# Layer 0 of a two-layer mixer and expert block: order of the output projection's column halves, and gathers in four buffers

## What is computed

```python
x = x + g1 * (concat(fourier, ssd) @ w_out)          # output projection, 1536 -> 1024, gated, residual
h2 = rms_norm(x) * (1 + sc2) + sh2
# PEER, for each token and each of 8 heads
q = h2 @ peer_wq                                     # two halves of 128
s = einsum(q, peer_keys); s_top, i_top = top_k(s, 16)
g_score, c_idx = top_k(s_top[0] + s_top[1], 16)      # 16 experts of 16384
act = gelu(u[experts] . h2) * softmax(g_score)
x = x + g2 * sum(act * v[experts])
```

## Time and profile before

| what | before |
|---|---|
| median of 3 runs | 4402.59 us (4401.46 to 4406.03) |
| the profiled execution | 4409.58 us, its span 4407.5 us |
| busy: TensorE, VectorE, ScalarE, GpSimd | 3129.8, 2860.7, 1122.0, 1587.9 us |
| bytes moved by the gathers | 1342.26 of 1471.78 MB |
| layer 0's first gather issued | at 720.9 us of the span |
| chain that ended last, largest share | DMA of experts, 13% |

### The profile page before, as it was taken

How to read it: one execution, slowest core, us unless ns; L and a number is a source line. 1 busy time by engine, 2 the same in 40 slices (tenths; PEclk the granted TensorE clock), 3 DMA queues, 4 the chain that set the end, 5 groups by cost and what they waited for, 6 DMA issues and landing times. The chain is left out here.

```text
span 4407.5 us, 37632 instructions
## 1 busy us (share of the span) xinstructions
PE 3129.8 (71%) x12112; PEld 1329.6 (30%) x12112; DVE 2860.7 (65%) x7084; ACT 1122.0 (25%) x2966; POOL 1587.9 (36%) x1383
## 2 busy tenths in 40 slices
PE   7999997676666765656666666999876755555555
PEld 4655554332222321111222222565432311111111
DVE  2524843988888887555555555565788899555554
ACT  1122521322322332111222211564322322111111
POOL 0002401545444444444444441001344454444443
PEclk9999998888887887776777878999987877777677
DMA  4114734999999999999999996103999999999998
GB/s 172 39 39 153 256 104 176 412 420 421 420 418 397 414 421 421 421 420 414 412 416 421 416 420 256 39 1 121 383 420 420 418 421 416 422 420 420 419 420 337
DMA packets 223656, 1471.78 MB, mean 334 GB/s; under 512 B 25436, under 2 KB 29244, under 8 KB 53220
## 3 DMA queue, kind: packets, MB, share of 16 engines
q0 software_dynamic: 184320, 1342.26, 73.5%
q1 hardware_dynamic: 37764, 123.17, 7.8%
q10 hardware_dynamic: 1376, 3.96, 0.2%
HBM read 1467.02 MB, written 2.28 MB: 333 GB/s over the span
## 5 line engine op out<-in xcount | busy, mean ns | idle before, releaser
L1868 PE MATMUL banks<-arena 128*64 128x512 f32 x5120 | 1688.5, 821 | 1206.0 <-ACT arena L2038 1148.9
L1670 POOL DMA_INDIRECT arena<-experts,arena x1280 | 1511.6, 1181 | 2309.8 <-PE banks L1868 1474.9
L2198 DVE CUSTOM_DVE_ANT_0 arena<-arena 128x1024 f32<-128x1024 f32 x1280 | 1535.4, 1224 | 793.1 <-DMA arena<-experts,arena 788.1
L1868 PEld LDWEIGHTS banks<-arena 128*64 128x64 f32 x5120 | 462.7, 187 | 2358.0 <-ACT arena L2038 1338.8
L2032 ACT ACTIVATE arena<-arena 128x4 f32<-128x4 f32 x320 | 66.0, 206 | 2334.3 <-DVE arena L2198 2319.4
L2038 ACT ACTIVATE arena<-arena 128x64 f32<-128x64 f32 x1280 | 340.6, 336 | 36.4
L1756 PE MATMUL banks<-arena 128*128 128x512 f32 (+3 forms) x960 | 289.0, 455 | 7.0 <-DMA arena<-wq 6.4
L434 PE MATMUL banks<-arena 128*128 128x512 f32 (+1 forms) x640 | 208.6, 486 | 1.8 <-PEq L201 1.8
L1756 PEld LDWEIGHTS banks<-arena 128*128 128x128 f32 x960 | 160.8, 191 | 113.3 <-issue 86.9
L870 POOL TENSOR_TENSOR arena<-arena 128x256 f32<-128x256 f32 x48 | 41.1, 856 | 423.6 <-POOLq L625 332.3
L1689 PE MATMUL banks<-arena 128*128 128x512 f32 x416 | 185.8, 600 | 2.3 <-PEq L953 1.5
(11 more groups left out here) (250 smaller groups left out, 3004.0 us busy)
## 6 DMA issues: line engine op xcount, KB each, us to landing
arena<-l_w_ada SPq DMA_DIRECT2D x48, 1024.0 KB, 5.0
arena<-wq SPq DMA_DIRECT2D x54, 512.0 KB
arena<-experts,arena POOLq DMA_INDIRECT x1280
arena<-l_w_in SPq DMA_DIRECT2D x7, 2048.0 KB, 7.8
arena<-l_w_out SPq DMA_DIRECT2D x4, 1536.0 KB, 8.9
arena<-l_w_o SPq DMA_DIRECT2D x4, 1024.0 KB, 9.9
arena<-keys SPq DMA_DIRECT2D x27, 128.0 KB
arena<-gates SPq DMA_DIRECT2D x6, 512.0 KB, 6.2
```

What stands on the lines that cost most here:

```text
L1670: pool.indirect_dma_start(slots[n], None, tbl, bass.IndirectOffsetOnAxis(ap=expert[:, ring[c], k:k + 1], axis=0)).then_inc(land[n]["sem"], ...
L1868: mm = pe.matmul(core["ps"][QS * j:QS * j + QS, c, :], diag[:, g % 2, k, :], v[:, D + c * 512:D + (c + 1) * 512], start=(g % (NB * PH) == ...
L2198: dve.tensor_tensor_reduce(u, u, rep[i // PH % 2][:, k % NQ, :], 1.0, 0.0, ALU.mult, ALU.add, dots[:, k:k + 1]).then_inc(dot["sem"], up(dot))
```

## The change

Only `peer_block` and its two tables change. The order of projection halves becomes a list, `project`, and `turn_of[t, c]` is a half's place in it. Layer 1's list is the old order, and its `spread_at` has a new meaning (start step for tile 0, for later tiles), which gives the same steps 4 and 5. In layer 0:

- halves run (0,0), (0,1), then the first halves of tiles 1 to 5, then the second halves of tiles 1 to 5;
- projections use PSUM banks 6 and 7 in turn, and the gate's transposes move to banks 2 to 5;
- the first 16 gathers use four slots only: three over the first column half's weights, and one that lies elsewhere. They wait for the first seven halves. From gather 16 on, 12 slots are used, and the 8 new ones wait for all halves, as before;
- `project(1, 1)` stands ahead of the loop on TensorE, and `project(2, 1)` to `project(5, 1)` after its steps 0 to 3, with the turned rows of tiles 1 to 4 behind them. `ask(2)` moves to step 1, `ask(3)` and `turn_rows(5)` to step 4;
- on VectorE the sums, norms and columns of tiles 1 to 5 move between the dot batches in the same way, and on ScalarE the squares, roots and columns;
- choices inside the loop begin at step 3 instead of 1; the spread of tile 1's rows is at steps 5 and 6 instead of 1 and 2.

```diff
@@ -1360,17 +1360,20 @@
-     "choose_from": 1, "spread_at": (1, 2), "small": 12, "ring_from": 0,
+     "choose_from": 3, "spread_at": (5, 1), "small": 4, "ring_from": 16,
+     "project": [(0, 0), (0, 1)] + [(t, 0) for t in range(1, TT)] + [(t, 1) for t in range(1, TT)],
      "rep": (L0 + 3072, L0 + 5120), "ht": HO,
-     "slots": [RO + n * ROWS for n in range(6)] + [L0] + [L0 + 7168 + n * ROWS for n in range(5)]},
+     "slots": [RO, RO + ROWS, RO + 2 * ROWS, L0 + 7168] + [RO + n * ROWS for n in range(3, 6)] +
+              [L0] + [L0 + 7168 + n * ROWS for n in range(1, 5)]},
...
@@ -1413,7 +1416,8 @@
-    REP_AT = m["spread_at"]
+    rep_at = {NB * PH * t + m["spread_at"][t > 0] + j: (t + 1, j) for t in range(tiles - 1) for j in range(NQ)}
+    turn_of = {tc: n for n, tc in enumerate(m["project"])}
...
@@ -1579,13 +1583,13 @@
-    def bank_of(c):
-
-        return c if layer == 0 else 6 + c
+    def bank_of(t, c):
+
+        return 6 + turn_of[t, c] % 2
     def spread_place(c):
 
-        return (3, 384 + 32 * c) if layer == 1 and c < EARLY else (6 + c % 2, 0)
+        return (3, 384 + 32 * c) if c < EARLY else (6 + c % 2, 0)
...
@@ -1645,10 +1649,10 @@
-                sp.wait_ge(free["sem"], at(free, max(used[n][1] for n in range(3)) + 1))
+                sp.wait_ge(free["sem"], at(free, max(used[n][1] for n in (0, 1, 2)) + 1))
...
@@ -1663,10 +1667,12 @@
                     uses, prev = before[u]
                     if uses:
                         pool.wait_ge(free["sem"], at(free, prev + 1))
-                    elif layer == 0 or n >= m["small"]:
+                    elif n >= m["small"]:
                         pool.wait_ge(omm["sem"], at(omm, 2 * tiles))
                         if layer == 0:
                             pool.wait_ge(oad["sem"], at(oad, 2 * tiles))
+                    elif layer == 0:
+                        pool.wait_ge(omm["sem"], at(omm, turn_of[tiles - 1, 0] + 1))
                     pool.indirect_dma_start(slots[n], None, tbl,
                                             bass.IndirectOffsetOnAxis(ap=expert[:, ring[c], k:k + 1], axis=0)
                                             ).then_inc(land[n]["sem"], up(land[n], 16))
...
-                elif layer == 1:
-                    pe.wait_ge(oad["sem"], at(oad, 2 * t + c - 1))
                 else:
-                    pe.wait_ge(oad["sem"], at(oad, 2 * (t - 1) + c + 1))
+                    pe.wait_ge(oad["sem"], at(oad, turn_of[t, c] - 1))
...
@@ -1812,54 +1825,59 @@
+                turn_rows(0)
+                project(2, 0, 0, 2)
+                pe.wait_ge(gca["sem"], at(gca, TT - 1))
+                pe.wait_ge(gcv["sem"], at(gcv, TT - 1))
+                query(0, 0)
+                query(0, 1)
+                project(2, 0, 2, 3)
+                scores(0, 0)
+                scores(0, 1)
+                project(2, 0, 3, K)
+                spread_rows(0, 0)
+                project(3, 0, 0, K // 2)
+                spread_rows(0, 1)
+                spread_choice(0)
+                project(3, 0, K // 2, K)
+                project(4, 0, 0, K // 2)
+                query(1, 0)
+                query(1, 1)
+                project(4, 0, K // 2, K // 2 + 1)
+                scores(1, 0)
+                scores(1, 1)
+                project(4, 0, K // 2 + 1, K)
+                project(5, 0)
+                project(1, 1)
             else:
                 project(0, 0)
                 project(0, 1)
                 project(1, 0)
...
-            if layer == 0:
-                for t in range(3, tiles):
-                    project(t, 0)
-                    turn_rows(t - 1)
-                    if t == 3:
-                        spread_choice(1)
-                    project(t, 1)
-                ask(2)
+                turn_rows(0)
...
             for g in range(POS):
                 i = g // NB
                 pe.wait_ge(dg["sem"], at(dg, g + 1))
-                if g == 0 and layer == 0:
-                    pe.wait_ge(oad["sem"], at(oad, 2 * tiles))
-                elif g and g % (NB * PH) == 0:
+                if g and g % (NB * PH) == 0:
...
-                if g == 0:
-                    if layer == 0:
-                        ask(3)
-                        turn_rows(tiles - 1)
-                    else:
-                        project(3, 0)
+                if g == 0 and layer == 0:
+                    project(2, 1)
+                    turn_rows(1)
+                    spread_choice(1)
+                if g == 1 and layer == 0:
+                    ask(2)
+                if 1 <= g < 4 and layer == 0:
+                    project(g + 2, 1)
+                    turn_rows(g + 1)
+                if g == 4 and layer == 0:
+                    ask(3)
+                    turn_rows(5)
+                if g == 0 and layer == 1:
+                    project(3, 0)
...
-            if layer == 0:
-                for t in range(2, tiles):
-                    squares(t)
-                    root(t)
-                    if t < tiles - 1:
-                        low_columns(t)
-                answer(2)
             for g in range(POS):
                 diagonals(g)
                 if half_at(g - 1) and half_at(g - 1)[1] == 0:
                     softmax(half_at(g - 1)[0])
-                if g == 0 and layer == 0:
-                    answer(3)
-                    low_columns(tiles - 1)
+                if layer == 0 and g < 5:
+                    squares(g + 1)
+                    root(g + 1)
+                    if g == 1:
+                        answer(2)
+                    if g == 4:
+                        answer(3)
+                    low_columns(g + 1)
...
@@ -2264,37 +2291,43 @@
                 gate_high(2)
             dve.wait_ge(gr["sem"], at(gr, 16 * conds))
             gate_out(0, 0)
+            gate_out(0, 1)
             if layer == 0:
                 gate_high(3)
                 gate_high(4)
-            gate_out(0, 1)
             norm_rows(0)
             if layer == 0:
                 gate_high(5)
             gate_out(1, 0)
             high_columns(0)
             choose_a(0)
-            choose_b(0)
-            gate_out(1, 1)
-            choice_out(0)
-            norm_rows(1)
-            gate_out(2, 0)
-            high_columns(1)
             if layer == 0:
+                gate_out(2, 0)
+                choose_b(0)
+                choice_out(0)
+                gate_out(3, 0)
+                gate_out(4, 0)
                 choose_a(1)
-                gate_out(2, 1)
+                gate_out(5, 0)
                 choose_b(1)
-                for t in range(3, tiles):
-                    norm_rows(t - 1)
-                    gate_out(t, 0)
-                    high_columns(t - 1)
-                    if t == 3:
-                        choice_out(1)
-                    gate_out(t, 1)
-                norm_rows(tiles - 1)
+            else:
+                choose_b(0)
+                gate_out(1, 1)
+                choice_out(0)
+                norm_rows(1)
+                gate_out(2, 0)
+                high_columns(1)
             gate_identity(0)
             for g in range(POS):
                 dot_batch(g)
+                if layer == 0 and g < 5:
+                    if g < 4:
+                        gate_out(g + 1, 1)
+                    norm_rows(g + 1)
+                    if g < 3:
+                        high_columns(g + 1)
+                    if g == 0:
+                        choice_out(1)
...
@@ -2319,8 +2352,10 @@
                         choose_a(c)
                     else:
                         choose_b(c)
-                if g == 0 and layer == 0:
-                    high_columns(tiles - 1)
+                if layer == 0 and g == 3:
+                    gate_out(5, 1)
+                if layer == 0 and 3 <= g < 5:
+                    high_columns(g + 1)
```

More of the change, by code:

```diff
@@ L1372 @@
               [(h, t) for h in range(4) for t in range(1, 4)] + [(h, t) for t in range(2, 4) for h in range(4, PH)],
-     "choose_from": 3, "spread_at": (4, 5), "small": 8, "ring_from": 16,
+     "choose_from": 3, "spread_at": (4, 4), "small": 8, "ring_from": 16,
+     "project": [(t, c) for t in range(TL) for c in range(2)],
      "w": RO + SLOT, "g1": HO + 16384, "g2": HO + 17408,
@@ L1733, in spread_choice @@
                     pe.wait_ge(gtd["sem"], at(gtd, c - 1))
-                if layer == 1 and c < 2:
-                    pe.wait_ge(sev["sem"], at(sev, 2 + 4 * c))
-                elif layer == 1 and c < 4:
+                if c < 2:
+                    pe.wait_ge(sev["sem"], at(sev, 2 + (2 + 2 * layer) * c))
+                elif c < 4:
                     pe.wait_ge(oad["sem"], at(oad, 2 * tiles))
@@ L1750, in query @@
                     pe.wait_ge(sev["sem"], at(sev, 2 * e - 1 + side))
-                if layer == 1 and side == 1 and e in (1, 3):
-                    pe.wait_ge(gtd["sem"], at(gtd, (e + 1) // 2))
```

(53 more changed lines are left out.)

33 lines of the change are left out of this document (18 added, 15 removed).

## The result

The changed kernel takes 4424.59 us (median of 6 runs, 4419.75 to 4426.47) where the kernel before, on the same chip, takes 4405.11 us (6 runs): ratio 1.0043, 95% interval 1.0033 to 1.0053, that is 15 to 23 us more. The profiled execution took 4424.62 us, its span is 4422.7 us against 4407.5, 15.2 us more.

The account below looks back on a forecast made before the run. Layer 0's gather stage was taken as bound by DMA bytes from the first gather on. All 12 slots open 62.9 us later against a credit of 43.0: +19.9 us on the median 4402.6, 4422 us, range 4408 to 4433.

Parts of the forecast that it names:

- T: Layer 0, the time at which all 12 gather slots open: 720.9 us before, forecast 783.8 after the change.
- first gather issued: GpSimd in layer 0: gather 0 issued at 663.9 us, after TensorE's earlier work ends at 663.0.
- landing of the fourth: First batch of four gathers: the fourth lands 14.4 us after the first issue; 17.4 would add 3.
- steps 0, 1, 2: Layer 0 loop, closed chain through matmuls, projection, turned rows, columns and dot products: 25.0, 34.2 and 24.8 us.
- one batch of loop matmuls: TensorE, a step's 16 records after about 7.5 us of idle time: 6.0 us, low end 3.65.
- step 3 to T: Step 3's matmuls 6.0, last projection 10.3, its sum and GpSimd's reaction: 18.8 us in all.
- credit of 16 gathers and the loads: Transfer moved ahead in layer 0: 40.2 us for 16 gathers plus 2.8 for wq and key loads, 43.0 us.
- The reordering at nothing: Halves reordered on TensorE ahead of the first gather: costs nothing; unseen waits for sums perhaps 5 us.
- What binds is the order, the transfer just hidden: Steps 0 to 2: next gathers land some 18 us after the matmuls' start, dot products cannot begin before 18.7.
- the head start wins: Rival: dot products run while TensorE projects, so its own work sets T, at 743.4; 4382 us, chance 0.08.
- A second gap behind T: Rival: ScalarE and VectorE work in step 4 makes step 5's slots late by up to 10 us; 4432, chance 0.07.
- The delay is absorbed: Rival: layer 0's stage catches up, or cheap steps and early landing cut the loss; 4403 to 4411, chance 0.10.

Follow-up runs that it names:

- order_only: Changed kernel without the early gathers: 12 slots wait for all halves, all projections ahead of the loop, new half order kept; 4409.79 us, ratio 1.0004 to before.
- warm: Changed kernel plus seven needless matmuls in TensorE's idle time ahead of the loop matmuls in each of steps 0 to 3; 4418.73 us, ratio 1.0029 to before.
- turn_first: Changed kernel with a tile's turned rows ahead of the projection in steps 0 to 3 instead of behind it; 4407.69 us, ratio 0.9997 to before.
- woven: Changed kernel with two second halves and tile 1's turned rows ahead of the loop, event 2's scores spread over the gaps; 4382.29 us, ratio 0.9942 to before.
- last_early: Changed kernel with the last projection and its sum in step 2 instead of step 3; 4418.73 us, ratio 1.0021 to before.
- both: Changed kernel with turned rows ahead of the projections and the last projection in step 2; 4404.89 us, ratio 0.9996 to before.
- both_fifth: Changed kernel with turned rows first, last projection in step 2, and tile 5's turned rows ahead of its scores in step 4; 4399.33 us, ratio 0.9985 to before.

## Why the prediction was right

The time (4422 forecast, 4424.59 measured) and the mechanism came out as forecast: an early start that is paid for with a late T. That the two times lie within 3 us is in part luck, since the interval of the ratio spans 9 us and the two profiled executions differ by 16.4 us at the last gather. Step by step, with its own terms:

| term | forecast | measured |
|---|---|---|
| first gather issued | 663.9 | 665.99, in a stage that began 2.4 later |
| landing of the fourth | 14.4 | 14.4 (665.99 to 680.38) |
| steps 0, 1, 2 | 25.0, 34.2, 24.8 | 25.5, 33.8, 24.7 |
| one batch of loop matmuls | 6.0 | 6.55, 5.74, 5.89, 5.48 |
| step 3 to T | 18.8 | 18.2 |
| T later by | 62.9 | 62.0 |
| credit of 16 gathers and the loads | 43.0 | 45.6 (from T to the last gather 1967.9 us before, 1922.3 after) |
| total | +19.9 | +19.5 by the medians, +16.4 at the last gather of the profiled executions |

The credit is the one term that was clearly off, by 2.6 us, and that is no accident of one execution. From T to the last gather it takes 1967.9 us in the kernel before and 1968.2 in order_only, the two that gather nothing early, but 1922.3 in the changed kernel, 1922.9 in warm, 1922.7 in turn_first and 1921.8 in woven. The largest difference is in one stretch. In the columns of the earlier trace rows, before, order_only and after:

```profile
1260.00:1460.00 200.00, 139.68 (x568) 53.94 (x568) 172.14 (x519) 57.57 (x142) 88.13 (x73) 0.83 0.98 403
...
1260.00:1460.00 200.00, 139.67 (x566) 54.11 (x564) 170.81 (x515) 56.76 (x142) 88.71 (x74) 0.83 0.98 400
...
1260.00:1460.00 200.00, 129.94 (x504) 47.16 (x504) 176.86 (x529) 53.09 (x135) 101.56 (x78) 0.81 1.00 412
```

At 417 GB/s, 403 instead of 412 over 200 us is 4.3 us, and the other six kernels with early gathers move 409 to 413 there. Part of it lies where the loop goes on to another tile: from 1400 to 1500 the DMA share is 0.96 and 0.95 in the first two, 0.97 or 0.98 in the others. The programs behind T are also less alike than the prediction's "From T on, the program is that of before, four steps on". The choices, and with them the queries and scores of later heads, which are placed by the choices, come two steps later in the loop than before, not four, and order_only has the old steps. Whether this shift makes the difference was not tested.

**The reordering at nothing:** right, by order_only. **What binds is the order, the transfer just hidden:** right; the dot products of steps 1 to 3 began with their gathers landed, and in turn_first, where they wait for the landing instead, the two steps that it binds are only 4.5 and 4.7 us shorter. **The clock:** the measured middle of a batch, 5.9 us, is about the 6.0 that the prediction took. The stretches of the changed kernel show where it comes from (granted clock in the third column from the right, 0.50 for 1.2 GHz and 1.00 for 2.4):

```profile
683.10:688.90 5.80, 5.80 (x14) 1.68 (x16) 0.92 (x2) 2.61 (x4) 1.58 (x2) 0.50 0.09 16
689.00:699.90 10.90, 10.90 (x28) 4.62 (x25) 0.00 (x0) 0.00 (x0) 2.06 (x3) 1.00 0.91 375
```

In step 0 nearly the whole batch (683.06 to 689.54) runs at the low level, and the projection behind it at the high one; in step 1 the level rises at about 712.8, 4.2 us into the batch. 16 records wholly at the low clock would take 6.8 us, an estimate from the Trainium skill ("TensorE: Matmul & The Clock Gate", section "Wait — 56ns, not 53.3ns?"). The trace agrees: the measured 5.48 to 6.55 lie between that and the 3.65 of 2.4 GHz, nearer to the low clock's end.

**The rival "the head start wins"** was priced at a T of 743.4 if TensorE's own work set it. In the changed kernel it did not; in woven it does, and T came at 739.7. Its total, 4382 us, is woven's time, but that they agree so closely is luck: woven is 25 us below its kernel before, where the rival had 20.5. The rule to issue early and wait late (the Trainium skill, "DMA: Bandwidth & Descriptors", section "Rules for kernel authors") is kept by both kernels. It pays in woven and loses in the changed kernel, because there the work put between stands in a closed chain with the next issue.

**"A second gap behind T"** did not come in the changed kernel: the share is 1.01 from 805 to 824 and 1.00 from 824 to 834. But such a gap does come once T is early: it cost 5.4 us in last_early and 6 us in both. The prediction named `choose_b(2)` and the norm as its cause; in the run both, VectorE had done these by 788.9 and then waited 7.2 us for the turned rows of tile 5 behind `ask(3)`, and both_fifth, which moves them ahead, loses 2 us instead of 6. **"The delay is absorbed"** did not come either.

## What to carry to other kernels

When a transfer-bound stage is given a head start, compare two numbers: the transfer time that is moved ahead, and how much later the point comes at which the full set of buffers opens. With few buffers each batch is a closed chain through all engines, and every instruction that stands in it ahead of what frees the next buffer is paid for, until the landing of the next batch binds (here at about 21 us a step): look first for a short step (here eight transposes, and the copies behind them) that stands behind a long one it does not need. Then fill the long engine's gaps with its own remaining work, which also holds its clock.

## What I had not expected

Moving T earlier does not pay in full by itself. The 16 gathers that GpSimd issues in the first 31 us behind T are 40 us of transfer (16 x 2.51), and the next ones wait for the slots of step 5. Where those came 43.3 us behind T (changed) the share of the like stretch was 1.00; at 45.0 (turn_first) it was 0.87, at 46.2 (both_fifth) 0.82, at 49.2 (last_early) 0.55 and at 49.9 (both) 0.48. And a saturated stretch is not the same in each kernel: 403 and 400 GB/s without early gathers, 409 to 413 with them. A difference that looks like one execution's noise is worth looking up in another kernel that shares that part of the program: here order_only repeats the slow stretch of the kernel before.
